# One level of Strassen's method for the two products of an MLP, in a float32 decoder layer on one core

## The reference

```
hid = relu(einsum('btd,df->btf', rms_norm(x, norm2_g), w_up))     # 2048 -> 8192
x = x + einsum('btf,fd->btd', hid * hid, w_down)                  # 8192 -> 2048
```

## Time and profile before

| | |
|---|---|
| median of 3 runs | 2503.01 us (2502.96 to 2503.69) |
| span of the profiled execution | 2501.7 us |
| TensorE busy | 2473.2 us, 99% |
| VectorE busy | 1334.8 us, 53% |
| ScalarE busy | 914.0 us, 37% |
| GpSimd busy | 257.6 us, 10% |
| moved by DMA | 352.39 MB, mean 141 GB/s |

### The profile page before, as it was taken

How to read it: one execution, slowest core, us unless ns; L and a number is a source line. 1 busy time by engine, 2 the same in 40 slices (tenths; PEclk the granted TensorE clock), 3 DMA queues, 4 the chain that set the end, 5 groups by cost and what they waited for, 6 DMA issues and landing times.

```text
span 2501.7 us, 40629 instructions
## 1 busy us (share of the span) xinstructions
PE 2473.2 (99%) x16734; PEld 2303.5 (92%) x16734; DVE 1334.8 (53%) x1883; ACT 914.0 (37%) x1584; POOL 257.6 (10%) x443
## 2 busy tenths in 40 slices
PE   8999999999999999999999999999999999999999
PEld 7999999755655599999999999999999999999999
DVE  6354455354435586455564464564554554554555
ACT  6244456432333444233333332233332332332333
POOL 0170000345454300000000000000000000000000
PEclk9999999999999999999999999999999999999999
DMA  6322233799999852222222222222222222222222
GB/s 187 117 95 88 85 103 105 267 384 362 375 366 373 300 188 85 87 100 85 85 87 93 91 85 85 102 85 85 88 95 88 85 85 100 86 85 86 100 85 106
DMA packets 96314, 352.39 MB, mean 141 GB/s; under 512 B 22361, under 2 KB 25050, under 8 KB 72578
## 3 DMA queue, kind: packets, MB, share of 16 engines
q1 hardware_dynamic: 65762, 250.68, 28.9%
q0 software_dynamic: 30368, 99.12, 10.6%
HBM read 337.69 MB, written 12.07 MB: 140 GB/s over the span
## 4 chain that ended last, share of the span: by engine, by line
PE 95%; DVE 3%; DMA 1%; ACT 1%; issue 1%; SPq 0%; ACTq 0%; DVEq 0%
PE bank L475 54%; PE bank L480 27%; PE bank L2130 3%; PE bank L2105 3%; PE bank L2065 2%; PE bank L2007 1%; DMA w_raw<-weights 1%; PE bank L1907 1%; PE bank L2036 1%; PE bank L2113 1%; PE bank L2021 1%; PE bank L2010 0%; DVE d_r L1649 0%; PE bank L2058 0%; PE bank L2074 0%
## 5 line engine op out<-in xcount | busy, mean ns | idle before, releaser
L475 PE MATMUL bank<-x_act,w_hi 128*128 128x364 f32 (+1 forms) x4800 | 1045.5, 328 | 1.2 <-DVE w_lo L466 1.1
L475 PEld LDWEIGHTS bank<-x_act,w_hi 128*128 128x128 f32 x4800 | 763.1, 188 | 2.8 <-DVE w_lo L466 1.4
L475 PE MATMUL bank<-hid,w_hi 128*128 128x364 f32 (+1 forms) x3456 | 719.4, 328 | 2.0 <-DVE hid L569 1.2
L480 PE MATMUL bank<-x_act,w_lo 128*128 128x272 f32 x3200 | 642.6, 287 | 0.0
L564 DVE TENSOR_TENSOR sum_tmp<-sum_tmp,bank 128x544 f32<-128x544 f32 x336 | 241.9, 720 | 684.1 <-ACT sum_tmp L558 684.1
L480 PEld LDWEIGHTS bank<-x_act,w_lo 128*128 128x128 f32 x3200 | 554.8, 188 | 2.9 <-issue 1.3
L475 PEld LDWEIGHTS bank<-hid,w_hi 128*128 128x128 f32 x3456 | 554.8, 188 | 2.7 <-issue 2.7
L557 ACT ACTIVATE sum_tmp<-bank 128x184 f32<-128x184 f32 x336 | 108.6, 323 | 1009.3 <-PE bank L475 1009.3
L480 PE MATMUL bank<-hid,w_lo 128*128 128x272 f32 x2304 | 429.0, 287 | 1.4 <-DVE hid L569 1.4
L466 DVE TENSOR_TENSOR w_lo<-w_raw,w_hi 128x2048 fp32r<-128x2048 f32 x171 | 392.0, 2293 | 28.7 <-ACT w_hi L449 28.5
L480 PEld LDWEIGHTS bank<-hid,w_lo 128*128 128x128 f32 x2304 | 378.0, 188 | 2.3 <-DVE hid L569 1.9
(11 more groups left out here) (251 smaller groups left out, 1542.2 us busy)
## 6 DMA issues: line engine op xcount, KB each, us to landing
w_raw<-weights SPq DMA_DIRECT2D x171, 1024.0 KB, 4.8
v_ring<-sb_v POOLq DMA_DIRECT2D x128, 256.0 KB, 5.1
v_ring<-fox_v POOLq DMA_DIRECT2D x120, 256.0 KB, 4.9
k_ring<-fox_k SPq DMA_DIRECT2D x64, 256.0 KB, 7.4
k_ring<-fox_k POOLq DMA_DIRECT2D x64, 256.0 KB, 4.4
k_ring<-sb_k SPq DMA_DIRECT2D x64, 256.0 KB, 10.6
k_ring<-sb_k POOLq DMA_DIRECT2D x64, 256.0 KB, 7.8
wo<-w_early SPq DMA_DIRECT2D x16, 512.0 KB, 9.7
```

The lines of the kernel that those rows point to most:

```text
L475: ins = nc.tensor.matmul(bank[:, base + b, 0:n], hi, row[:, t:t + n], start=begin, stop=end)
L480: ins = nc.tensor.matmul(bank[:, base + b, 0:HALF], lo, row[:, t:t + HALF], start=False, stop=False)
```

## The change

A Strassen step (in Winograd's form) splits both factors of a product into 2 x 2 blocks and computes the result from seven products of block sums instead of eight products of blocks. Here the weights are split by contraction half and by output block, the activations by contraction half and by token half (2 x 272). Both products of the MLP are done so.

- The work is cut into 80 units, 32 for the up product and 48 for the down product. A unit makes two row blocks of output (256 features x 544 tokens). It has seven products P1, P2, P6, P5, P7, P4, P3; each is `depth` steps deep, and a step is three matmuls of 272 columns (high x high, high x low, low x high). An up unit is 8 steps deep. The down product's 32 hidden blocks are passed over by windows: a unit covers 5 or 6 blocks of a row pair (6 units, then, make up one pair of output row blocks).
- Before the up product the activations get a preparation: all 16 row blocks are normalised (the factor is now applied before the product), four differences of quarters are made, and seven operands of 8 x 272 columns are split into high and low parts.
- Per unit VectorE makes four sums or differences of weight blocks (`sum_1` to `sum_4`) and seven low parts, ScalarE seven high parts. These go through a ring of four buffers, so the parts for product n + 4 can be made from the end of product n.
- Three of the banks are copied by ScalarE (`copy_line`), VectorE adds them to the others (`first_ends`, `second_ends`). In an up unit relu and squares follow on ScalarE; VectorE makes the four differences of the hidden block, ScalarE and VectorE their high and low parts.
- The hidden blocks (7 operands x 2 parts x 272 columns x 128 partitions, 1.95 MB each) go to DRAM (`hid_parts`) and come back, seven buffers of them, for the down product. The residual goes to DRAM (`res`) and comes back in pairs of rows, to which `join_a` and `join_b` add the down units' results.
- Weights are laid out anew in the host's arrays `w_up` and `w_down`, and come in blocks of up to 512 KB, six buffers deep.

The core of the diff:

```diff
+P1, P2, P6, P5, P7, P4, P3 = range(7)
+RUN = []
+for _v in range(UNITS_MLP):
+    RUN += [(_v, P1), (_v - 1, P3)] if _v not in (0, UP_UNITS) else [(_v - 1, P3)] * (_v > 0) + [(_v, P1)]
+    RUN += [(_v, _o) for _o in (P2, P6, P5, P7, P4)]
+RUN.append((UNITS_MLP - 1, P3))
...
     @block.sync
+        for v in range(UNITS_MLP):
+            for b in range(4):
+                m = 4 * v + b
+                i, _ = piece_slot(v, b)
+                if m >= RAW:
+                    for before in held.get(m - 4 * UP_UNITS, (m - RAW,)):
+                        sp.wait_ge(*freed(before))
...
+                sp.dma_start(raw(v, b), src).then_inc(raw_in[i].s, 16)
...
     @block.gpsimd
+        def store_hidden(u):
+            pool.wait_ge(*hid_ready.at(u + 1))
+            pool.dma_start(hid_parts[u, :, 0], hid_h[:].bitcast(F32)).then_inc(hid_stored, 16)
+            pool.dma_start(hid_parts[u, :, 1], hid_f[:]).then_inc(hid_stored, 16)
...
+        for u in range(LAST):
+            store_hidden(u)
+        for i in range(HID_SLOTS):
+            load_hidden(i)
+            if i in (1, 3):
+                load_rows(i // 2)
...
     @block.scalar
+        def first_squares(v):
+
+            act.wait_ge(*a_relu.at(v + 1))
+            if v:
+                act.wait_ge(hid_stored, 32 * v)
+            f(hid_f[:, 0:7:6], ends_a[:], ACT.Square).then_inc(a_squared.s, 1)
...
+        for n, (v, o) in enumerate(RUN):
+            if o == P1:
+                copy_line(v, n, ROOT_LINE)
+            if o == P6:
+                copy_line(v, n, MID_LINE)
+            if o == P7:
+                copy_line(v, n, TOP_LINE)
+            if n + RING < len(RUN):
+                op_high_part(n + RING)
+            if o == P4 and v < UP_UNITS:
+                first_relu(v)
+            if o == P3 and v < UP_UNITS:
+                first_squares(v)
+                second_squares(v)
+            if o == P6 and 1 <= v <= UP_UNITS:
+                hidden_high(v - 1)
...
     @block.vector
+        for t in range(HALF_K):
+            normed_row(t)
+        dve.wait_ge(*x_normed.at(HALF_K))
+        mixed(P5, quarter(0, 1), quarter(0, 0))
+        x_low(P1, quarter(0, 0))
+        for t in range(HALF_K, KT):
+            normed_row(t)
...
+        mixed(P6, quarter(1, 1), x_dif[P5][:])
+        x_low(P2, quarter(1, 0))
+        mixed(P7, quarter(1, 1), quarter(0, 1))
...
+        mixed(P4, quarter(1, 0), x_dif[P6][:])
+        for o in (P6, P5, P7):
+            x_low(o, x_dif[o][:])
...
+        x_low(P4, x_dif[P4][:])
+        x_low(P3, quarter(1, 1))
+        op_low_part(RING - 1)
...
     @block.tensor
-        up(C_MLP, T_MLP, split=KT, between=mean_square)
...
+        mean_square()
...
+            for k in range(depth(u)):
...
+                cols = slice(P * k, P * k + P)
+                mm(out, part_of(n, 0)[:, cols], high, start=(first and k == 0), stop=False, skip_group_check=True)
+                mm(out, part_of(n, 0)[:, cols], low, start=False, stop=False, skip_group_check=True)
+                ins = mm(out, part_of(n, 1)[:, cols], high, start=False, stop=(k == last), skip_group_check=True)
+            ins.then_inc(product_done.s, 1)
```

More of the change, by code:

```diff
@@ L1321, in _, with op_source @@
-        down(CHUNKS - 4, T_LAST, KT * FF_CHUNKS, last=True)
+        root(act, own, n2_tmp[3][:], J_2, KT)
+        def op_source(o):
+            if o in x_dif:
+                return x_dif[o][:]
+            k0, h = {P1: (0, 0), P2: (HALF_K, 0), P3: (HALF_K, 1)}[o]
+            return x_res[:, k0:k0 + HALF_K, HALF * h:HALF * h + HALF]
+        for n, (o, s, count) in enumerate(((P1, x_normed, 8), (P2, x_normed, KT), (P6, x_mixed, 2), (P5, x_mixed, 1),
+                                           (P7, x_mixed, 3), (P4, x_mixed, 4), (P3, x_normed, KT))):
+            act.wait_ge(*s.at(count))
+            f(x_op[o][:, 0], op_source(o), ACT.Copy).then_inc(x_op_high.s, 1)
@@ L1834, in down @@
-        def down(c0, t0, i=0, step=0, last=False, rows=None):
-            per = step * 40 // 16
-            for j in range(4):
-                for m in range(4):
-                    n = t0 + 4 * j + m
-                    sum_tile(dve, halves(sum_tmp[n % 2][:]), n, per, i)
-                    if m == 0 and not (last and j == 3):
-                        low_part(dve, c0 + j + 1, i, step)
-                    add_to_x(4 * j + m, n, per, i)
-                    if rows and j == 0 and m == 1:
-                        dve.wait_ge(hid_h, rows[0] + 4 + step // 2 * i)
-                        low_parts(hid[:, rows[1], 3], n2_tmp[1][:], hid_l)
@@ L1858, in _ @@
+        join_b(UNITS_MLP - 1)
     @block.tensor
@@ new lines, in product @@
+        def product(n):
+            u, o = RUN[n]
+            pe.wait_ge(*op_low.at(n + 1))
+            if o == P1 and u >= 2:
+                pe.wait_ge(*line_copied.at(3 * (u - 1)))
+            if o in (P2, P5, P4) and u >= 2:
+                pe.wait_ge(*combined.at(2 * (u - 1)))
+            if o == P6:
+                pe.wait_ge(*line_copied.at(3 * u + 1))
+            if o == P7:
+                pe.wait_ge(*line_copied.at(3 * u + 2))
+            if o == P3:
+                pe.wait_ge(*combined.at(2 * u + 1))
+            if u == 0:
+                pe.wait_ge(*x_op_low.at(o + 1))
+            k0 = window(u - UP_UNITS)[0] if u >= UP_UNITS else 0
+            out = bank[:, 4 * (u % 2) + BANK[o], 0:HALF]
+            first, last = o in (P1, P2, P5, P4), depth(u) - 1
+            for k in range(depth(u)):
+                if u < UP_UNITS:
+                    high, low = x_op[o][:, 0, k], x_op[o][:, 1, k]
+                else:
+                    i = k0 + k
+                    if o == P1:
+                        pe.wait_ge(*hid_loaded[i % HID_SLOTS].at(16 * (i // HID_SLOTS + 1)))
+                    high, low = hid_in[i % HID_SLOTS][:, 0, o], hid_in[i % HID_SLOTS][:, 1, o]
+                cols = slice(P * k, P * k + P)
[3 more added lines that the diff above has]
+            ins.then_inc(product_done.s, 1)
@@ L2224, in build_step @@
+        for n in range(len(RUN)):
+            product(n)
     ctx.close()
```

415 lines of the change are left out of this document (296 added, 119 removed).

## The result

| | before | after |
|---|---|---|
| median | 2502.99 us (2502.93 to 2503.69, 4 runs) | 2426.89 us (2424.55 to 2429.03, 4 runs) |
| span of the profiled execution | 2501.7 us | 2422.8 us |
| TensorE busy | 2473.2 us, 99% | 2318.0 us, 96% |
| VectorE busy | 1334.8 us, 53% | 1652.3 us, 68% |

The ratio is 0.9695 (95% interval 0.9681 to 0.9709): 76 us, 3.0% faster. Forecast were 2423 us and 3.2%.

What follows compares the result with a forecast made beforehand. TensorE's matmuls were taken to bound the MLP. Of 191 us gained there, 83 went to the two seams, 19 to the VectorE-ScalarE loop and 8 to late weights: 2423 us, 3.2% faster; 8-in-10 range 2388 to 2490.

Steps and rivals of the forecast that it cites:

- two seams: MLP's start and turn from up to down part, where TensorE idles: 40 and 2, and 41 us lost.
- TensorE's pace: MLP: 0.1225 us per matmul of 272 columns, 10,752 of them; with waits 1334 us, 191 less than before.
- the term of 19 us: Up part: VectorE and ScalarE waiting for each other make a unit 21.4 us, 0.6 above TensorE; 19 us in all.
- the walk: One up unit followed step by step: VectorE's own 19.4 us plus 1.8 of waits for ScalarE, 21.2 us.
- The MLP's start: Before the first up products: TensorE waits for normalised rows and operands made by VectorE; 40 us lost, 2 more for slow clock.
- The turn: From up to down part: hidden-block loads queue behind block 30's store, 14 MB at 370 GB/s; 41 us lost.
- Late weights: Down part: the fourth weight block may land late while a hidden block loads; 8 us taken, up to 68 possible.
- Rival 2: Late data sets the pace: fourth weight blocks and slower stores; 2524 us at worst, 2475 with both at half; 20%.
- 1: Rival: weight loads keep the MLP's narrow matmuls 0.135 us apart; 2538 us, slower; 6%.
- 3: Rival: no loop between VectorE and ScalarE, up units 20.8 us, no late weights, turn 33 us; 2386 us; 14%.

Runs made afterwards that it cites:

- narrow: The change's kernel with all MLP matmuls except the first of a bank streaming 256 columns instead of 272; 2421.72 us, one execution.
- extra3: The change's kernel with three more VectorE sums of weight blocks (1024 elements, 1.22 us each) per up unit; 2475.03 us, one execution.
- late: The change's kernel with each load of a hidden block in the down part held back for two more products; 2402.55 us, ratio 0.9597 against the kernel before.

## Why the prediction was right

Its core held: fewer products on TensorE, two seams of some 30 to 40 us each, and neither engine nor transfers in the way of most of the MLP. 191 us less work were forecast, 80 of them kept; about 79 us of span were kept. By its own steps:

**TensorE's pace: mis-sized by 2 to 3%.** Forecast 0.1225 us for a matmul of 272 columns, from 0.49/4 between the starts of rows 3. Measured 0.1261 in the up part (1100 to 1600 us) and 0.1251 in the down part (1800 to 2300, waits left out), here in nine starts of one product:

```profile
1024.05 0.29 PE L2535 MATMUL bank<-x_op,ring 128*128 128x272 f32 x1
...
1025.05 0.29 PE L2537 MATMUL bank<-x_op,ring 128*128 128x272 f32 x1
```

Eight starts later 1.00 us has gone. That makes 12 us more than forecast in the up part and 4 in the down part. The row misled since its last gap was that to a wide matmul: in the trace of before, from 1200 to 2400 us, a narrow matmul starts 124.4 ns ahead of a narrow one and 122.1 ahead of a wide one. A whole step of before tells it better: from rows 3, two steps' parts (4 narrow, 3 wide) take 1045.87 - 1044.88 = 0.99 us for 2176 columns, 0.455 ns a column against 0.417 at 2.4 GHz: 0.084 us over, 12 ns for each of the seven. 272/2.4 + 12 = 125 ns, the down part's pace, 1 below the up part's. The Trainium skill (TensorE: Matmul & The Clock Gate, "Back-to-back issue gap") gives 116 ns here, for the isolated gap; measured are 12 ns over the columns in place of its 2.5. The section also says, as the prediction did not, that the formula is off for a stream with a weight load per matmul, and gives 131 ns at 512 columns; that does not hold here either, since the wide matmuls of rows 3 took 0.167 us each.

**VectorE and ScalarE: the term of 19 us did not exist.** The step that failed is "instructions in a row lie 0.03 to 0.04 apart", and the walk built on it. Durations per pass were right (1.22 us at 1024, 2.135 at 1904). But passes that don't depend on each other start before the one in front has ended. Rows of VectorE in the down part after:

```profile
1868.08 0.95 DVE L1993 TENSOR_TENSOR ring<-down_raw,ring 128x768 fp32r<-128x768 f32 x1
1868.95 0.95 DVE L2016 TENSOR_TENSOR down_raw<-down_raw,down_raw 128x768 f32<-128x768 f32 x1
1869.82 0.95 DVE L1993 TENSOR_TENSOR ring<-down_sum,ring 128x768 fp32r<-128x768 f32 x1
```

0.87 us apart, each 0.95 long: 0.08 less instead of 0.04 more. Rows 6, from which I took the gap, are a chain in which each reads what the last wrote. A unit is 17.6 us of VectorE (83% of 21.2), not 19.4, and the loop ends up shorter than TensorE's 21.2: `narrow` shows it at or below 19.84, `extra3` at 22.7 with 3.6 us more. The trace of before showed the overlap elsewhere, a pass and the next:

```profile
44.79 2.29 DVE L466 TENSOR_TENSOR w_lo<-w_raw,w_hi 128x2048 fp32r<-128x2048 f32 x1 [0.45 <-ACT w_hi L449]
47.00 0.17 DVE L1364 TENSOR_SCALAR derived<-par 128x8 f32<-128x8 f32 x1
```

The second starts 0.08 us before 44.79 + 2.29 = 47.08. The Trainium skill (VectorE: DVE Perf Modes, "The DRAIN you can't avoid") says that the next instruction does not start before the pipeline is empty, and that one that is not held starts earlier; these rows, in which one starts 0.08 us before the end of the one ahead, agree with the second. Forecast and measurement of the up unit (21.4 and 21.2) agree by accident: a term that was too short on TensorE and one that did not exist on VectorE.

**The MLP's start: right.** 46.3 us against 49.4, with the holes where they were forecast: 18.5 us with the matmul of ones in it (forecast 19), then 5.48, 5.11 and 2.62 (forecast 8, 4.5 and 8). They are shorter in part because the products ahead of them ran slow. The clock falls there: after the hole of 11.98 the matmuls start 0.226 apart (1.2 GHz) for 3.5 us, then 0.126; likewise behind the holes of 5.48, 5.11 and 2.62, where the forecast of the clock knew only one slow product. Each slow spell of 16 matmuls costs 1.6 us, but those of the first three products only shorten the holes behind them; the one of the fourth, 12 matmuls or 1.2 us, counts (forecast 2).

**The turn: mechanism right, size 12 us too long.** The first load stands behind the store of block 30, as forecast, and the DMA engines are full. But the DMA engines moved 430 GB/s from 1699.04 to 1719.84 us, where I took the 370 of the attention stage; the store left 4.9 us before the up part's end instead of 2; and of the 4 us added for joins and a slow restart none came as a wait of its own. The slow restart came later, in the next line of the table: matmuls 0.226 apart to 1722.7 and for 3.4 us from 1736.4, 2.4 us together. So the 370 was no limit. That smaller pieces (256 KB transfers there) made the difference is possible but wasn't tried.

**Late weights: right in kind, 8 forecast, 20.6 measured in waits and 24 with the 0.24 us more behind each.** The forecast leant on the mean DMA share. The mean (0.56) says nothing here: the request in question is made within 0.5 us of one five times its size. 15 times VectorE waited, 3.5 us on average (52.5 in all), and its slack took more than half of that. Rival 2 is thus what happens with the weights, at a third of its price. Its estimates of 6.5 us for a store and 2.8 for a weight block come near where nothing stands in the way (6.6 from first issue to last landing, and 3.2 for 320 KB), though the fit behind them is for GpSimd's transfers and weights come by SyncE; "so no stall" left out the block in the other queue.

**Rivals.** 1 (weight loads set the pace at 0.135) is refuted by 0.126 and by 0.118 in `narrow`. 2 holds for weights and not for the store: ScalarE's squares waited for it twice in the whole run, 2.9 us together, and the up part has no wait of TensorE. 3 had the loop term right (0) and the turn nearly (33 for 30.6), but no late weights and the pace of 0.1225; with 24 and 16 us for these its 2386 would be 2426.

## What to carry to other kernels

When two queues ask within a microsecond of each other, the one that somebody waits for soon must ask first: one number in a wait was worth 24 us here, and the mean DMA share showed nothing of it. Take an instruction's pace from a row in which only its own kind follows itself, and an engine's gap from rows with the dependences that the new code will have: chained passes and independent ones differ by 0.12 us each, 10% of a pass. And when a forecast total comes out right, compare its marks along the way; here four terms were wrong by 12 to 19 us (pace 16 and late weights 16 too short, loop 19 and turn 12 too long) and their sum by 1.

## What the runs showed of the hardware

- A matmul of 272 columns with its own weight load costs 12 to 13 ns over its columns at 2.4 GHz (125.1 and 126.1 for 113.3) and nothing at 1.2 GHz (0.226 for 0.2267). So at the high clock something that does not follow the columns is in the way, but it is no floor: at 256 columns the pace is 0.118. The cause stays open.
- The length of a hole alone did not tell whether the clock fell to 1.2 GHz behind it. Rows of `narrow`: behind the first the matmuls start 0.213 us apart (256 columns at 1.2 GHz are 0.2133) for 20 starts, then 0.118; behind the second, a longer hole than the 2.62 that slowed the change's fourth product, they start 0.118 apart at once.

```profile
1785.39 0.55 PE L2537 MATMUL bank<-hid_in,ring 128*128 128x256 f32 x1 [4.16 <-DVE ends_a L2092]
...
2279.95 0.35 PE L2537 MATMUL bank<-hid_in,ring 128*128 128x256 f32 x1 [3.29 <-DVE ends_a L2092]
```

- Transfers of whole hidden blocks (15 KB per partition) moved 430 GB/s at the turn (1699.04 to 1719.84 us); the kernel before showed 370 in its attention stage, and at most 384 in any of the 40 slices of its page.
- A block of 384 KB lands in 3.6 us (median) in `late`, and in 7.9 in the change's kernel. With a 1.9 MB load requested half a microsecond earlier in another queue it lands just after it, as here from 1899 to 1909 us (KB each, us from issue to landing):

```profile
hid_in<-hid_parts POOLq DMA_DIRECT2D x1, 1904.0 KB, 8.4
...
down_raw<-w_down SPq DMA_DIRECT2D x1, 384.0 KB, 8.1
```

  Issued at 1899.22 and 1899.72, they land at 1907.6 and 1907.8. In all twelve such pairs whose landings the profile holds, from 1768 us on, the weight block lands 0.2 to 0.4 us after the hidden block. The Trainium skill (DMA: Bandwidth & Descriptors, "Queues, rings and completion order") says that an engine takes turns between queues by packet. Both transfers have 128 packets in the trace, of 15,232 and of 3072 bytes; taking turns packet by packet they would end together, and they do.
